# Norms over heads and memory norm inside the q/k/v products, S5 tables on GpSimd, weight splits ahead of an attention

## The chip, the core and the metric

The kernel runs on one core of a Trainium2 chip as one launch. Its time is the device time of that core in microseconds. TensorE (PE) multiplies into eight PSUM banks, ScalarE (ACT), VectorE (DVE) and GpSimd (POOL) compute beside it, SyncE (SP) issues the transfers. All engines are ordered by semaphores alone. Each runs its instructions in program order.

## The reference, cut to what matters

Two transformer blocks over 256 tokens of width 1024 in fp32. The first block: an attention with a relative bias, an MLP, a sparse latent attention, an MLP, a norm. The second: a mixer of RWKV and S5 halves, cross attention to a memory, a gated MLP, differential attention, cross attention again, a mixture of experts. The parts that the change touches:

```python
def memory_cross_attention(h, mem_n, w_q, w_kv, q_gain, k_gain, w_o):
    q = rms_norm_2((h @ w_q).reshape(b, t, MEM_HEADS, MEM_HEAD_DIM), q_gain).astype(F32)      # 4 heads of 256
    k, v = jnp.split(mem_n @ w_kv, 2, axis=-1)                                               # mem_n = rms_norm_2(mem, norm_mem[l])
    k = rms_norm_2(k.reshape(b, m, MEM_HEADS, MEM_HEAD_DIM), k_gain).astype(F32)
...
def diff_attention(h, w_qkv, q_gain, k_gain, lam_q1, lam_k1, lam_q2, lam_k2, sub_gain, w_o, lambda_init):
    q, k, v = jnp.split(h @ w_qkv, 3, axis=-1)
    q = rms_norm_2(q.reshape(b, t, DIFF_HEADS, 2, DIFF_HEAD_DIM), q_gain).astype(F32)        # 16 groups of 64
    k = rms_norm_2(k.reshape(b, t, DIFF_HEADS, 2, DIFF_HEAD_DIM), k_gain).astype(F32)
```

S5 needs cos and sin of (step x angle) for 256 steps and 16 x 128 states; the kernel makes them by doubling a table, level by level.

## The kernel before, in words

The program is a chain of stages (`stage`), each a block with one function per engine and a barrier at its end. A stage's functions are written in the order in which each engine runs them; nothing is scheduled by a planner.

Weights come as tiles of 128 x 2048 fp32 (1 MB) through a ring of six. For precision each is split into a high part (`hi`, L280, ScalarE) and a low part (`lo`, L289, VectorE: tile minus high), two fp32r matrices whose products are added. Split tiles live in `WS`, which has `WS_BUFS = 2` buffers, so the high half of tile i waits until PE has used tile i-2:

```python
                if s >= WS_BUFS:
                    before = [j for j in range(i) if not self.tiles[j][1]][s - WS_BUFS]
                    act.wait_ge(self.filled.sem, self.tile_used[before])
```

`qkv_products` runs eight q/k products (u = 0 to 7, one tile each, 32 matmuls, L459 and L460) and four v tiles (24 matmuls each, L365). Behind product i ScalarE splits tile i+2 and copies the product's part with low activations (L1030), VectorE makes the low half and adds the parts into `qk` (L1042, `bank_copied`).

`grouped_norm` is a stage of its own behind it. ScalarE squares two tiles at a time (L757), PE sums them over the partitions of a head with a matrix of ones (L770, fp32), ScalarE and VectorE make one inverse root a head and token (L761, L789), PE spreads it back over partitions (L781, fp32), VectorE multiplies it with the gain onto q and k (L794). It serves both cross attentions, the differential attention, and others that don't change. A cross attention has ahead of its products: the norm of x (`norm_stage`), a stage that waits for the memory's transfer, and the same `norm_stage` on the memory.

`mlp` runs chunks of up (and gate) and down tiles. In the second MLP of the first block `beside` is the S5 object: `tables_dve` puts steps of the table on VectorE behind each tile, from tile 7 on the doublings (`double`, L2305). The stage of the latent attention that picks the top keys ends with copies on ScalarE and the selection on VectorE; `project`, behind the attention, needs two split tiles of the output weights.

## Time and profile before

| | us |
|---|---|
| median of 3 runs | 2943.56 |
| lowest, highest | 2926.44, 2945.67 |
| the profiled execution | 2930.94 |
| its span | 2929.1 |
| mean granted TensorE clock | 0.937 |
| PE busy | 2601.7 (89%) |
| VectorE, ScalarE, GpSimd busy | 1915.5, 1515.6, 90.4 |

The span is the time between the first and the last record on the core. A busy time is the sum of an engine's records; matmuls overlap, so 89% isn't PE at its peak. The granted clock is given as a share of 2.4 GHz; 0.5 is 1.2 GHz. Line numbers (L280) are those of the kernel before. "idle before" is the time in which an engine waited just ahead of that instruction, with whom it waited for.

### The profile page before, as it was taken

What the parts mean: (1) busy time and instruction counts of PE and PEld (TensorE: products, weight loads), DVE (VectorE), ACT (ScalarE), POOL (GpSimd) and SP (SyncE); (2) the same over time, 40 slices, a digit from 0 to 9 for tenths busy, and PEclk for the clock granted to TensorE, in tenths of its full rate; (3) what the DMA queues carried; (4) which work ended last, traced back from release to release, by engine and by line L of the source; (5) the groups of instructions that cost most, each with busy time, mean ns of one, the idle gap of its engine ahead of it and who ended that gap; (6) DMA issues with size and microseconds to landing.
All of it is one profiled execution on the core that took longest, in us unless ns stands there. A gap on an engine that the chain in (4) does not pass through costs nothing. (4 is left out here: it accounts for less than half of the span.)

```text
span 2929.1 us, 37611 instructions
## 1 busy us (share of the span) xinstructions
PE 2601.7 (89%) x13581; PEld 2117.6 (72%) x13582; DVE 1915.5 (65%) x2368; ACT 1515.6 (52%) x1875; POOL 90.4 (3%) x115
## 2 busy tenths in 40 slices
PE   6889887997869698998978879998998999999998
PEld 5678765776765486887757657777887777777777
DVE  4555545796668544555455459885454889888888
ACT  3544335443221343444444347774443777777776
POOL 0000011000143000000100000000000000000000
PEclk9999988998887898999989879999998999999999
DMA  8346512455200541464414239995554899999996
GB/s 276 133 153 191 164 58 94 144 179 164 68 2 1 201 158 58 159 198 147 144 40 147 72 115 365 327 361 188 183 182 152 313 319 348 330 357 330 358 328 225
DMA packets 333583, 566.24 MB, mean 193 GB/s; under 512 B 21929, under 2 KB 126712, under 8 KB 333080
## 3 DMA queue, kind: packets, MB, share of 16 engines
q1 hardware_dynamic: 333464, 564.59, 56.9%
q8 instruction: 83, 1.36, 0.2%
q14 instruction: 36, 0.29, 0.0%
HBM read 561.19 MB, written 6.50 MB: 194 GB/s over the span
## 5 line engine op out<-in xcount | busy, mean ns | idle before, releaser
L1240 DVE TENSOR_TENSOR weights_split<-ring,weights_split 128x1024 fp32r<-128x1024 f32 x676 | 819.3, 1224 | 266.5 <-ACT weights_split L1235 229.2
L1315 PE MATMUL ps<-weights_split,expert_split 128*128 128x512 f32 x3864 | 914.6, 394 | 25.9 <-DVE expert_split L1411 17.7
L1235 ACT ACTIVATE weights_split<-ring 128x1024 fp32r<-128x1024 f32 x676 | 715.3, 1061 | 353.1 <-PE ps L1315 341.8
L1315 PEld LDWEIGHTS ps<-weights_split,expert_split 128*128 128x128 f32 x3864 | 722.3, 189 | 193.2 <-DVE weights_split L1240 38.2
L289 DVE TENSOR_TENSOR weights_split<-ring,weights_split 128x2048 fp32r<-128x2048 f32 x182 | 413.4, 2272 | 418.0 <-ACT weights_split L280 417.4
L280 ACT ACTIVATE weights_split<-ring 128x2048 fp32r<-128x2048 f32 x182 | 345.0, 1896 | 436.4 <-PE ps L460 259.0
L459 PE MATMUL ps<-normed_split,weights_split 128*128 128x512 f32 x1248 | 446.4, 400 | 25.5 <-PEq L342 25.1
L460 PE MATMUL ps<-normed_split,weights_split 128*128 128x256 f32 x1248 | 353.7, 283 | 0.0
L459 PEld LDWEIGHTS ps<-normed_split,weights_split 128*128 128x128 f32 x1248 | 239.6, 192 | 82.1 <-issue 27.5
L365 PE MATMUL ps<-weights_split,hidden_split 128*128 128x512 f32 x1032 | 244.4, 393 | 17.4 <-DVE weights_split L289 9.3
L460 PEld LDWEIGHTS ps<-normed_split,weights_split 128*128 128x128 f32 x1248 | 239.9, 192 | 1.4
L365 PEld LDWEIGHTS ps<-weights_split,hidden_split 128*128 128x128 f32 x1032 | 191.8, 189 | 61.4 <-issue 12.4
L365 PE MATMUL ps<-weights_split,normed_split 128*128 128x512 f32 (+1 forms) x816 | 197.4, 403 | 26.0 <-DVE normed_split L586 18.8
L365 PEld LDWEIGHTS ps<-weights_split,normed_split 128*128 128x128 f32 x816 | 157.2, 198 | 65.4 <-issue 20.9
L1315 PE MATMUL ps<-weights_split,normed_split 128*128 128x512 f32 x672 | 159.1, 397 | 0.0
L1315 PEld LDWEIGHTS ps<-weights_split,normed_split 128*128 128x128 f32 x672 | 126.1, 189 | 30.2
L527 ACT ACTIVATE hidden_split<-arena 128x512 fp32r<-128x512 f32 x43 | 27.2, 633 | 150.7 <-DVE arena L554 115.5
L365 PE MATMUL ps<-normed_split,weights_split 128*128 128x256 f32 (+2 forms) x576 | 73.3, 291 | 9.1 <-PEq L342 7.5
L365 PEld LDWEIGHTS ps<-normed_split,weights_split 128*128 128x128 f32 (+2 forms) x576 | 72.2, 194 | 10.7 <-issue 8.6
L659 PE MATMUL ps<-const,arena 128*128 128x128 f32 x176 | 38.7, 410 | 44.5 <-DVE arena L640 44.5
L659 PEld LDWEIGHTS ps<-const,arena 128*128 128x128 f32 x176 | 34.7, 217 | 48.8 <-DVE arena L640 48.8
L781 PE MATMUL ps<-arena 8*128 8x256 f32 (+2 forms) x120 | 45.5, 562 | 12.9 <-DVE arena L789 12.9
(393 smaller groups left out, 2339.0 us busy)
## 6 DMA issues: line engine op xcount, KB each, us to landing
ring<-moe_w_gate SPq DMA_DIRECT2D x112, 1024.0 KB, 5.2
ring<-moe_w_up SPq DMA_DIRECT2D x112, 1024.0 KB, 5.3
ring<-moe_w_down SPq DMA_DIRECT2D x112, 1024.0 KB, 5.2
ring<-mlp_w_up SPq DMA_DIRECT2D x32, 1024.0 KB, 5.5
ring<-mlp_w_down SPq DMA_DIRECT2D x32, 1024.0 KB, 5.0
ring<-xa_w_kv SPq DMA_DIRECT2D x16, 1024.0 KB, 5.2
ring<-moba_w_qkv SPq DMA_DIRECT2D x12, 1024.0 KB, 12.2
ring<-da_w_qkv SPq DMA_DIRECT2D x12, 1024.0 KB, 5.2
```

The costliest lines, as they stand in the source:

```text
L280: self.nc.scalar.activation(self.half(i, 0), self.ring_tile(i), ACT.Copy).then_inc(*self.hi_done.up())
L289: self.nc.vector.tensor_tensor(self.half(i, 1), self.ring_tile(i), self.half(i, 0).bitcast(F32), ALU.subtract).then_inc(*self.lo_done.up())
L365: ins = core.nc.tensor.matmul(out, lhs, rhs, start=(first and n == 0), stop=(last and n == len(PASSES) - 1))
L459: core.nc.tensor.matmul(out, w[0][w_at], xs[:, :, k, :], start=first, stop=False)
L460: return core.nc.tensor.matmul(out[:, 0:T], w[1][w_at], xs[:, 0, k, :], start=False, stop=last)
L527: nc.scalar.activation(HS[:, c % 2, 0].rearrange("p k t -> p (k t)"), h[:, c % 2, :], ACT.Copy)\
L659: last = nc.tensor.transpose(core.ps[:, k // 2, k % 2 * T + tt * P:k % 2 * T + (tt + 1) * P], xs[:, tt, k * P:(k + 1) * P], core.c("ident"))
L781: last = nc.tensor.matmul(ps[:, 1 + u % 3, j * T:(j + 1) * T], ones[:, k * P:(k + 1) * P], inv, start=True, stop=True)
L1235: nc.scalar.activation(split_piece(p, 0), ring_piece(p), ACT.Copy).then_inc(high.sem, 1)
L1240: nc.vector.tensor_tensor(split_piece(p, 1), ring_piece(p), split_piece(p, 0).bitcast(F32), ALU.subtract)\
L1315: last = nc.tensor.matmul(ps[:, banks[half][tt], :], stationary(s, k, tt), split_piece(p, i)[:, kk * NW:(kk + 1) * NW], start=(opens and n ...
```

## The change

The two cross attentions and the differential attention use a new function, `qkv_normed`, in place of `qkv_products` and `grouped_norm`. `per_unit == 1` (`one`) is the cross attention, with heads of 256; there VectorE first adds the two squares of a product (`both`, `halves_added`) and PE sums once (`pick`). With heads of 64 PE sums twice. The inverse roots are kept as 32 or 64 rows of a high part above as many of a low one, so that a single fp32r matmul spreads them (`spread_unit`); those of q are made behind product 4, those of k behind the first v tile. In a cross attention the memory is normed at the head of this stage, beside product 0, and transposed by PE behind it; the waiting stage and the memory's `norm_stage` go. In the differential attention the lambda steps lead the stage, and GpSimd makes the slopes' table in it.

The S5 doublings go from VectorE to GpSimd (`tables_pool`), each linked to the one before it. The stage ahead of the latent attention splits two tiles of the output weights at its end.

```diff
         e.dma_start(mem, w["mem_2"][0].rearrange("(t p) d -> p t d", p=P)).then_inc(*mem_landed.up(16))
     norm_stage(core, core.x, core.XS, at_col("norm_xattn_2", 8 * layer), 0, extra_sp=sp)
-    def sp(e):
-        e.wait_ge(*mem_landed.at(0))
-    stage(core, sp=sp)
     qk = a(0, 16 * T).rearrange("p (n t) -> p n t", t=T)
     vN = a(4096, TT * D).rearrange("p (t d) -> p t d", t=TT)
     oT = a(6144, 8 * T).rearrange("p (n t) -> p n t", t=T)
     SCR = 8192
-    with core.scoped("memory_split", [P, 2, KD, T], F32R) as MS:
-        norm_stage(core, mem, MS, at_col("norm_mem_2", 8 * layer), 0)
-        qkv_products(core, core.XS, MS, qk, vN, None)
     def gain(j):
         which, r = at_col("xa_q_gain_2" if j < 8 else "xa_k_gain_2", 2 * layer)
         return core.cols[:, which, r + j % 2:r + j % 2 + 1]
-    gpe, gact, gdve = grouped_norm(core, qk, 16, MD, "norm_xattn", gain, SCR)
-    stage(core, pe=gpe, act=gact, dve=gdve)
+    def mem_gain(k):
+        which, r = at_col("norm_mem_2", 8 * layer + k)
+        return core.cols[:, which, r:r + 1]
+    with core.scoped("memory_split", [P, 2, KD, T], F32R) as MS:
+        qkv_normed(core, 1, gain, qk, vN, (mem, MS, mem_gain, mem_landed))
     q, k = qk[:, 0:8, :], qk[:, 8:16, :]
...
+def qkv_normed(core, per_unit, gain, qk, vN, memory=None, lead=None, pool=None):
...
+    SUMS, SPREAD = 6, (7, 7, 7, 7, 7, 2, 3, 6)
+    v_bank = lambda half, tt: 4 * (1 - half) + tt
+    mem, MS, mem_gain, mem_landed = memory or (None, core.XS, None, None)
...
+    def pe(e):
+        def pick(u):
+            cols = slice(u // 4 * T, u // 4 * T + T)
+            if u == 0 and memory:
+                e.wait_ge(*mem_split.at(4))
+            if u == 4:
+                e.wait_ge(*roots.at(1))
+            if one:
+                e.wait_ge(*halves_added.at(u + 1))
+                first = u % 4 + 1
+                last = nc.tensor.matmul(ps[0:R, SUMS, cols], c("pick_all")[:, PICK - first:PICK - first + R],
+                                        both[:, u % 2, :], start=(u % 4 == 0), stop=(u % 4 == 3))
+            else:
+                e.wait_ge(*squares.at(u + 1))
+                first = 2 * (u % 4)
+                for t in range(2):
+                    last = nc.tensor.matmul(ps[32 * t:32 * t + 32, SUMS, cols],
+                                            c("pick")[:, PICK - first:PICK - first + 32],
+                                            sq[:, u % 2, t * T:(t + 1) * T], start=(u % 4 == 0), stop=(u % 4 == 3))
+            last.then_inc(*sums.up())
...
+        def spread_unit(j):
+            if j == 0:
+                e.wait_ge(*spreader_made.at(1))
+            if j % 4 == 0:
+                e.wait_ge(*inverse_.at(j // 4 + 1))
+            if 1 <= j <= 4:
+                e.wait_ge(*normed.at(j))
+            if j == 5:
+                e.wait_ge(*freed.at(8))
+            if j == 7:
+                e.wait_ge(*roots.at(2))
+            for t in range(2):
+                m = j % 4 if one else 2 * (j % 4) + t
+                last = nc.tensor.matmul(ps[:, SPREAD[j], t * T:(t + 1) * T], spreader[0:2 * R, m * P:(m + 1) * P],
+                                        split[0:2 * R, :], start=True, stop=True)
+            last.then_inc(*spread.up())
+        for u in range(8):
+            w = core.weights(e, t0 + u)
+            xs = core.XS if u < 4 else MS
+            if u >= 2:
...
+            if u == 4 and memory:
+                e.wait_ge(*mem_split.at(4))
+            for t in range(2):
+                for k in range(KD):
+                    last = wide_product(core, ps[:, 2 * (u % 2) + t, :], w, (ALL, k, slice(t * P, (t + 1) * P)),
+                                        xs, k, k == 0, k == KD - 1)
+            core.fill(last, bank=True, tile=True)
+            if u == 0 and memory:
+                for tt in range(TT):
+                    e.wait_ge(*mem_scaled.at(tt + 1))
+                    for k in range(KD):
+                        last = nc.tensor.transpose(ps[:, 4 + k // 2, k % 2 * T + tt * P:k % 2 * T + (tt + 1) * P],
+                                                   mem[:, tt, k * P:(k + 1) * P], c("ident"))
+                        if tt == TT - 1 and k % 2 == 1:
+                            last.then_inc(*mem_turned.up())
+            if u >= 1:
+                pick(u - 1)
+            if u >= 5:
+                spread_unit(u - 5)
+        for i in range(4):
+            half, j = i // 2, i % 2
+            if i == 2:
+                e.wait_ge(*freed.at(8))
+            w = core.weights(e, t0 + 8 + i)
+            for tt in range(TT):
+                for k in range(4):
+                    last = product(core, ps[:, v_bank(half, tt), :], w, (ALL, k, ALL), halves(MS),
+                                   (ALL, 4 * j + k, slice(tt * P, (tt + 1) * P)), j + k == 0, 4 * j + k == 7, tokens=True)
+                if j == 1 or tt == TT - 1:
+                    core.fill(last, bank=(j == 1), tile=(tt == TT - 1))
+            if i == 0:
+                pick(7)
+                spread_unit(3)
+            if i == 1:
+                spread_unit(4)
+            if i == 2:
+                for j in (5, 6, 7):
+                    spread_unit(j)
...
+    def act(e):
+        if lead:
+            lead.act(e)
+        if memory:
+            e.wait_ge(*mem_landed.at(0))
...
+        for i in range(12):
+            core.hi(e, min(t0 + i + 1 + WS_BUFS, t0 + 13))
+            if i < 8:
+                core.wait_bank(e, i)
+                if i >= 2:
+                    e.wait_ge(*freed.at(i - 1))
+                nc.scalar.activation(two(low[:, i % 2, :]), ps[:, 2 * (i % 2):2 * (i % 2) + 2, T:2 * T], ACT.Copy)\
+                    .then_inc(*low_kept.up())
+                e.wait_ge(*freed.at(i + 1))
+                if i >= 2:
+                    e.wait_ge(*(halves_added if one else sums).at(i - 1))
+                nc.scalar.activation(sq[:, i % 2, :], flat(qk[:, 2 * i:2 * i + 2, :]), ACT.Square).then_inc(*squares.up())
...
+            if i == 0 and memory:
+                for b in range(4):
+                    e.wait_ge(*mem_turned.at(b + 1))
...
+            if i == 4:
+                e.wait_ge(*sums.at(4))
+                nc.scalar.activation(root, ps[0:R, SUMS, 0:T], ACT.Sqrt, bias=eps(E_EPS256 if one else E_EPS64, R))\
+                    .then_inc(*roots.up())
+            if i == 8:
+                e.wait_ge(*sums.at(8))
+                nc.scalar.activation(root, ps[0:R, SUMS, T:2 * T], ACT.Sqrt, scale=1.0 / size, bias=eps(E_EPS, R))\
+                    .then_inc(*roots.up())
...
+    def dve(e):
+        def invert(phase):
+            e.wait_ge(*roots.at(phase + 1))
+            core.link(e, "dve", V.reciprocal(inv, root))
+            if phase:
+                e.wait_ge(*spread.at(4))
+            core.link(e, "dve", V.tensor_copy(split[0:R, :], inv))
+            V.tensor_tensor(split[R:2 * R, :], inv, split[0:R, :].bitcast(F32), ALU.subtract)\
+                .then_inc(*inverse_.up())
+        def apply(j):
+            e.wait_ge(*spread.at(j + 1))
+            if one:
+                for t in range(2):
+                    last = V.scalar_tensor_tensor(qk[:, 2 * j + t, :], qk[:, 2 * j + t, :], gain(2 * j + t),
+                                                  ps[:, SPREAD[j], t * T:(t + 1) * T], ALU.mult, ALU.mult)
+            else:
+                last = V.scalar_tensor_tensor(flat(qk[:, 2 * j:2 * j + 2, :]), flat(qk[:, 2 * j:2 * j + 2, :]),
+                                              gain(2 * j), ps[:, SPREAD[j], :], ALU.mult, ALU.mult)
+            last.then_inc(*normed.up())
+        if lead:
...
+        if memory:
+            e.wait_ge(*mem_landed.at(0))
...
+        for i in range(12):
+            core.lo(e, min(t0 + i + 1 + WS_BUFS, t0 + 13))
+            if one and 1 <= i <= 8:
+                u = i - 1
+                e.wait_ge(*squares.at(u + 1))
+                if u >= 2:
+                    e.wait_ge(*sums.at(u - 1))
+                V.tensor_tensor(both[:, u % 2, :], sq[:, u % 2, 0:T], sq[:, u % 2, T:2 * T], ALU.add)\
+                    .then_inc(*halves_added.up())
+            if i < 8:
+                e.wait_ge(*low_kept.at(i + 1))
+                V.tensor_tensor(qk[:, 2 * i:2 * i + 2, :], ps[:, 2 * (i % 2):2 * (i % 2) + 2, 0:T], two(low[:, i % 2, :]),
+                                ALU.add).then_inc(*freed.up())
+            if i == 0 and memory:
+                for b in range(4):
+                    e.wait_ge(*mem_high.at(b + 1))
+                    for j in range(2):
+                        k = 2 * b + j
+                        last = V.scalar_tensor_tensor(MS[:, 1, k, :], ps[:, 4 + b, j * T:(j + 1) * T], mem_gain(k),
+                                                      MS[:, 0, k, :].bitcast(F32), ALU.mult, ALU.subtract)
+                    last.then_inc(*mem_split.up())
+            if i in (4, 8):
+                invert(i // 4 - 1)
+            if 5 <= i <= 9:
+                apply(i - 5)
+            if i == 10:
+                for j in (5, 6, 7):
+                    apply(j)
+    stage(core, pe=pe, act=act, dve=dve, pool=pool, uses=12)
+    guard.__exit__(None, None, None)
...
-        if n == 7:
-            link = self.core.link
-            link(e, "dve", self.core.nc.vector.memset(self.COS[:, :, 0:1], 1.0))
-            link(e, "dve", self.core.nc.vector.memset(self.SIN[:, :, 0:1], 0.0))
-            self.double(e, 1, 0, ST)
-            self.double(e, 2, 0, ST)
-        if n == 8:
-            self.double(e, 4, 0, ST)
-            self.double(e, 8, 0, ST)
-        first = 9
-        for level in self.LEVELS[4:]:
...
+    def tables_pool(self, e):
+        g, link = self.core.nc.gpsimd, self.core.link
+        t1, t2 = self.qt
+        link(e, "pool", g.memset(self.COS[:, :, 0:1], 1.0))
+        link(e, "pool", g.memset(self.SIN[:, :, 0:1], 0.0))
+        e.wait_ge(*self.turn_made.at(1))
+        tt = lambda out, x0, x1, op: link(e, "pool", g.tensor_tensor(out, x0, x1, op))
+        q = (self.co, self.si)
+        for level in self.LEVELS:
             count = min(ST, 512 // level)
-            for group in range(ST // count):
-                for part in range(2):
-                    if n == first:
-                        self.double(e, level, group * count, count, (part,))
-                    first += 1
+            for first in range(0, ST, count):
+                which = slice(first, first + count)
+                x1, x2 = (t[:, 0:count * level].rearrange("p (s n) -> p s n", n=level) for t in self.tmp)
+                qc, qs = bc(q[0][:, which], 2, level), bc(q[1][:, which], 2, level)
+                COS, SIN = self.COS[:, which, :], self.SIN[:, which, :]
+                tt(x1, COS[:, :, 0:level], qc, ALU.mult)
+                tt(x2, SIN[:, :, 0:level], qs, ALU.mult)
+                tt(COS[:, :, level:2 * level], x1, x2, ALU.subtract)
+                tt(x1, COS[:, :, 0:level], qs, ALU.mult)
+                tt(x2, SIN[:, :, 0:level], qc, ALU.mult)
+                tt(SIN[:, :, level:2 * level], x1, x2, ALU.add)
+            if level < self.LEVELS[-1]:
+                q2 = (self.qc, self.qs) if q[0] is not self.qc else (self.qc2, self.qs2)
+                tt(t1, q[0], q[0], ALU.mult)
+                tt(t2, q[1], q[1], ALU.mult)
+                tt(q2[0], t1, t2, ALU.subtract)
+                tt(t1, q[0], q[1], ALU.mult)
+                tt(q2[1], t1, t1, ALU.add)
+                q = q2
...
+        core.hi(e, core.taken + 3 + WS_BUFS)
...
+        core.lo(e, core.taken + 3 + WS_BUFS)
...
-    qkv_products(core, core.XS, core.XS, qk, vN, None)
-    npe, nact, ndve = grouped_norm(core, qk, 16, 64, "norm_diff",
-                                   lambda j: col("da_q_gain_2") if j < 8 else col("da_k_gain_2"), SCR)
...
+    qkv_normed(core, 4, lambda j: col("da_q_gain_2") if j < 8 else col("da_k_gain_2"), qk, vN, lead=Lambda(), pool=pool)
```

The order of the instructions shows how this stands on the engines. The names are those of the tiles (`weights_split` the split weights, `ring` the landed ones, `arena` scratch, `ps` PSUM), and [waits ...] names semaphores. VectorE in the first cross attention's products, kernel before:

```order
L348 UNCONDITIONAL_BRANCH [waits barrier_Pool_Activation_PE_DVE_SP_release]
L289 TENSOR_TENSOR weights_split<-ring,weights_split 128x2048 [waits weights_high]
L1042 SCALAR_TENSOR_TENSOR arena<-ps,arena 128x512 [waits bank_low]
L289 TENSOR_TENSOR weights_split<-ring,weights_split 128x2048 [waits weights_high]
L1042 SCALAR_TENSOR_TENSOR arena<-ps,arena 128x512 [waits bank_low]
```

The same engine there, changed kernel, from the end of product 0's work (L1264 writes the memory's low half; L287 is what L289 was, L1257 what L1042 was):

```order
L1264 SCALAR_TENSOR_TENSOR memory_split<-ps,cols,memory_split 128x256
L287 TENSOR_TENSOR weights_split<-ring,weights_split 128x2048 [waits weights_high]
L1253 TENSOR_TENSOR arena<-arena 128x256 [waits group_squares]
L1257 TENSOR_TENSOR arena<-ps,arena 128x512 [waits bank_low]
L287 TENSOR_TENSOR weights_split<-ring,weights_split 128x2048 [waits weights_high]
```

The add of the squares, L1253, is new and stands between the low half of a tile and the add of that product. PE there, changed kernel, between products 1 and 2 (L457 and L458 are the product's matmuls, L1087 the sum over partitions):

```order
L457 MATMUL ps<-normed_split,weights_split 128x512
L458 MATMUL ps<-normed_split,weights_split 128x256
L1087 MATMUL ps<-arena,const 32x256 [waits group_halves]
L457 MATMUL ps<-normed_split,weights_split 128x512 [waits bank_copied,weights_split]
L458 MATMUL ps<-normed_split,weights_split 128x256
```

L1087 is new between two products, and waits for VectorE's L1253. ScalarE there, changed kernel (L278 is the high half, which waits for PE's `products`, L1175 the low activations' copy, L1180 the square):

```order
L278 ACTIVATE weights_split<-ring 128x2048 [waits products,weights_landed1]
L1175 ACTIVATE arena<-ps 128x512 [waits bank_copied,products]
L1180 ACTIVATE arena<-arena 128x512 [waits group_halves,bank_copied]
L278 ACTIVATE weights_split<-ring 128x2048 [waits products,weights_landed2]
L1175 ACTIVATE arena<-ps 128x512 [waits bank_copied,products]
```

The square is new behind the copy, and waits for VectorE.

## Rows read from the trace of the kernel before

Columns of a timeline row: start, duration in us, engine, line, operation, out<-in by tile, shapes, count, and idle time before it with its releaser. Columns of a window: the stretch, its length, then busy us (instructions) of PE, PEld, DVE, ACT and POOL, mean granted clock, share of the DMA engines, GB/s.

**Rows 1.** The page's costliest groups: busy, mean ns, idle before, releaser
```profile
L280 ACT ACTIVATE weights_split<-ring 128x2048 fp32r<-128x2048 f32 x182 | 345.0, 1896 | 436.4 <-PE ps L460 259.0
...
L460 PE MATMUL ps<-normed_split,weights_split 128*128 128x256 f32 x1248 | 353.7, 283 | 0.0
```
**Rows 2.** Windows: memory norm, norms over heads (cross, differential), attention's start, products
```profile
1015.10:1024.90 9.80, 3.67 (x16) 3.29 (x17) 6.20 (x14) 4.66 (x12) 0.00 (x0) 0.65 0.11 39
1094.20:1119.80 25.60, 21.13 (x64) 12.76 (x64) 9.93 (x18) 5.48 (x9) 0.00 (x0) 0.70 0.11 38
1442.80:1469.60 26.80, 20.49 (x64) 12.43 (x64) 10.66 (x24) 8.19 (x13) 10.04 (x8) 0.74 0.10 36
1119.80:1124.70 4.90, 4.83 (x12) 3.87 (x13) 0.69 (x1) 1.60 (x2) 0.00 (x0) 0.50 0.00 2
1024.90:1093.90 69.00, 68.38 (x352) 58.35 (x352) 30.02 (x19) 27.09 (x23) 0.00 (x0) 0.98 0.47 153
```
**Rows 3.** Timelines of ScalarE, then VectorE, in the cross attention's products
```profile
1037.92 1.92 ACT L280 ACTIVATE weights_split<-ring 128x2048 fp32r<-128x2048 f32 x1 [3.15 <-PE ps L460]
...
1043.47 1.92 ACT L280 ACTIVATE weights_split<-ring 128x2048 fp32r<-128x2048 f32 x1 [3.14 <-PE ps L460]
...
1039.87 2.29 DVE L289 TENSOR_TENSOR weights_split<-ring,weights_split 128x2048 fp32r<-128x2048 f32 x1 [2.65 <-ACT weights_split L280]
1042.08 0.68 DVE L1042 SCALAR_TENSOR_TENSOR arena<-ps,arena 128x512 f32<-128x512 f32 x1
```
**Rows 4.** Timelines: an add of 256 columns, and steps of the norms over heads
```profile
581.16 0.42 DVE L2305 TENSOR_TENSOR arena<-toep,arena 128x256 f32<-128x256 f32 x1
...
1094.93 7.14 PE L770 MATMUL ps<-arena,const 128*8 128x256 f32 x32 [1.64 <-ACT arena L757]
...
1096.00 0.63 ACT L757 ACTIVATE arena<-arena 128x512 f32<-128x512 f32 x1 [0.60 <-PE ps L770]
...
1102.70 1.74 DVE L789 RECIPROCAL arena<-arena 8x256 f32<-8x256 f32 x1 [7.21 <-ACT arena L761]
...
1453.00 1.28 ACT L761 ACT_TABLE_LOAD   x1
1454.30 0.56 ACT L761 ACTIVATE arena<-ps,const 32x256 f32<-32x256 f32 x1
```
**Rows 5.** PE's first product of the cross attention: its first matmul, its window
```profile
1024.91 0.47 PE L459 MATMUL ps<-normed_split,weights_split 128*128 128x512 f32 x1 [3.23 <-PEq L342]
...
1024.90:1032.40 7.50, 7.49 (x34) 6.51 (x35) 0.00 (x0) 0.02 (x1) 0.00 (x0) 0.77 0.01 2
```
**Rows 6.** Timeline of ScalarE: splits ten chunks apart in the two MLPs
```profile
224.69 1.92 ACT L280 ACTIVATE weights_split<-ring 128x2048 fp32r<-128x2048 f32 x1 [2.96 <-PE ps L460]
...
334.69 1.92 ACT L280 ACTIVATE weights_split<-ring 128x2048 fp32r<-128x2048 f32 x1 [2.96 <-PE ps L460]
...
567.41 1.91 ACT L280 ACTIVATE weights_split<-ring 128x2048 fp32r<-128x2048 f32 x1 [2.88 <-PE ps L460]
...
690.00 1.92 ACT L280 ACTIVATE weights_split<-ring 128x2048 fp32r<-128x2048 f32 x1 [2.96 <-PE ps L460]
```
**Rows 7.** Timelines of GpSimd and VectorE, alone and beside each other
```profile
429.79 0.73 POOL L2711 TENSOR_TENSOR dsa<-toep,dsa 128x256 f32<-128x256 f32 x1
...
871.32 0.69 DVE L2483 TENSOR_TENSOR ring<-toep,ring 128x512 f32<-128x512 f32 x1
...
881.99 1.11 POOL L2448 TENSOR_TENSOR ring<-ring 128x256 f32<-128x256 f32 x1
882.61 1.03 DVE L2483 TENSOR_TENSOR ring<-toep,ring 128x512 f32<-128x512 f32 x1
```
**Rows 8.** Timelines around the latent attention: ScalarE's last copy, the projection's start
```profile
427.60 0.60 ACT L2679 ACTIVATE arena<-ps 128x512 f32<-128x512 f32 x1 [1.12 <-PE ps L2869]
...
465.35 2.19 ACT L578 ACTIVATE normed_split<-arena 128x512 fp32r<-128x512 f32 x4 [0.34 <-PEq L342]
...
471.72 1.65 PE L365 MATMUL ps<-weights_split,normed_split 128*128 128x512 f32 x3 [7.14 <-DVE weights_split L289]
```

121 lines of the change are left out of this document (76 added, 45 removed).

## The prediction

> **What bounds the kernel now.** I read the page first. TensorE (PE) is 89% busy and ends nearly every step of the chain that ended last; the costliest ScalarE line, the high half of the weights' split (L280), spends 259 us idle behind PE's L460 [rows 1]. So in product stages PE sets the pace and the other engines have slack. Then I read the stages the change touches, by windows [rows 2]. In the first cross attention the memory norm takes 9.8 us, the q/k/v products 69.0, the norm over heads 25.6. The norm over heads before the differential attention takes 26.8 us. Those norm stages are chains across engines and PE's 21 busy us there are small matmuls. They are what the change wants inside the 69 us. The question is then what a product period leaves free. The timeline of a steady product shows it [rows 3]: ScalarE starts the split of the weights that come two products later when a product ends, at 1037.92, again 5.55 us on; VectorE has made the low half and starts what stands behind it at 1042.08, 4.16 us after the product's end. The two buffers of split weights make this so: the split can't start before the product ends.
>
> **The change, part by part.** *Cross attention (twice), gains.* The two norm stages go: 9.8 + 25.6 = 35.4 us. The scores behind them no longer start on a half clock (4.9 us at 0.50 [rows 2]): half of that, 2.4. Together 37.8.
>
> *Cross attention, costs.* (a) The memory's 16 transposes now stand in the middle of dense PE work: 3.67 us busy in the old stage, at a clock of 0.65 [rows 2], taken as 3.4. (b) The sum matmul of product u-1 stands in PE's queue between products u and u+1, and waits for `halves_added`. The order shows VectorE's add of the two squares, L1253, *behind* the low half of product u+2's weights, which waits for the high half, which waits for product u's end. So PE cannot pass the end of product u before split, add and sum are done. That is 4.16 (to the slot behind the split) + 0.42 (an SBUF add of 256 columns) + 0.45 (one sum: 7.14 us / 16 [rows 4]) + 0.3 for the handovers, an estimate: a high half ends at 1039.84 and its reader starts at 1039.87 [rows 3], and there are several such steps and the matmuls' own filling: 5.35. Behind the waiting sum in the queue stands the whole of product u+1, and behind that every engine. It occurs for u = 1 to 7 and once more behind the first v tile: 8 x 5.35 = 42.8 us. Its cover doesn't exist: the DMA, ScalarE and VectorE are all ahead or waiting for PE. (c) The clock. Before the first product PE sat idle 3.23 us, and that product ran 7.50 us at a mean clock of 0.77, against 5.55 after it at full clock [rows 3, 5]: 1.95 us lost. The new idle spells are 4.7 us long, so I charge 1.95 for each: 15.6 us. Bounds: nothing, and 5.55 (a whole product at 1.2 GHz). (d) 16 spreading matmuls, now single-pass fp32r: a 256-column one lasts 0.28 us [rows 1], overlapped, so about 0.2: 3.0. The old ones are gone with their stage. Squares (0.63), reciprocal (1.74) and the products with gains fit the slack that (b) makes. The sum per cross attention: 3.4 + 42.8 + 15.6 + 3.0 - 37.8 = 27.0, twice 54.0 us.
>
> *Differential attention.* Gone: 26.8, and half of the low clock behind it, estimated at 1.4. Here the squares are summed without L1253, and square u-1 is done 4.16 + 0.68 + 0.63 = 5.5 us after product u-1 [rows 3, 4], before product u ends, so there is no such wait. PE gets 16 sums x 0.45 = 7.1 and 3.0 of spreads. Once, the inverse is late: product 4 ends, then 5.5 to its square, a table load 1.28, root 0.56, reciprocal 1.74, two short copies of some 0.4 each: 9.9 [rows 4]; PE arrives after 5.55 + 2 x 0.89 = 7.3, and waits 2.6 (bounds 0 and 4), for which I take a clock loss of 1.9, and 0.9 at the second inverse. Sum: 7.1 + 3.0 + 2.6 + 1.9 + 0.9 - 28.2 = -12.7. GpSimd's slopes ran under the norm and now run under products that are four times as long.
>
> *S5 tables.* In the MLP without tables ten chunks take 110.0 us (224.69 to 334.69); beside the doublings 122.6 (567.41 to 690.00) [rows 6]. The most to gain is 12.6. GpSimd takes 0.73 us for 256 columns [rows 7], so at most 1.46 for 512; 42 such operations are 61 us, and the 65 smaller ones at about 0.3 another 20. These 81 us fit the ten chunks and the stage's rest if nothing holds them up. But VectorE and GpSimd do hold each other: L2483, an add of two SBUF tiles, takes 0.69 us alone and 1.03 beside a GpSimd operation, whose own time rises from 0.73 to 1.11 [rows 7]. Each chunk has four such VectorE operations (two splits, the squared relu, the hidden split), of which three are in a chain with some 0.6 us to spare; at 0.35 a piece that chain is 1.05 late, 0.45 too much. For about ten chunks: 4.6 us given back. I take -8.0 (bounds -12.6 and +8). The Trainium skill states the same as a lock ("SBUF — State Buffer", SBUF: two separate sides: the pair of ports is held for the whole instruction and the other side blocks). The rows agree with it; by the page alone GpSimd gets only what is left of a chunk by the VectorE operations with two SBUF inputs, and that is rival 3.
>
> *Splits ahead.* ScalarE's last copy of the stage before starts at 427.60 and takes 0.60; two splits behind it, with their low halves, move that stage's end by 5.7 us. The projection's first matmul comes 6.37 us after the stage's first copy (465.35 to 471.72) [rows 8] and can come after 1.5; PE's clock gains half a microsecond and loses one earlier. Net +1.0.
>
> **The sum.** 54.0 - 12.7 - 8.0 + 1.0 = +34.3 us. The profiled execution took 2930.9 us (span 2929.1 and 1.8 around it), which makes 2965.2. That execution is 12.6 us under the median of the runs (2943.56); the four together have a mean of 2936.7. I give the middle of what these suggest, **2970 us**.
>
> **Rivals.**
> 1. *The clock holds across the waits.* Against it: the 7.50 us product. For it: nothing says that a spell of 4.7 us between dense products does what 3.23 us between small ones did. Without 2 x 15.6 and 1.9 the sum is +1: 2938. Chance 0.13.
> 2. *The clock stays low.* Each product behind a wait runs at 1.2 GHz throughout, 5.55 more instead of 1.95, 16 times: +58, 3028. Chance 0.07. The Trainium skill describes such a loop ("TensorE: Matmul & The Clock Gate", HAM oscillation: a wait in each tile makes each burst run cold). The rows show a recovery inside one product.
> 3. *GpSimd becomes the bound of the S5 stage.* Split, relu and hidden split hold VectorE 4 times a chunk; if GpSimd gets less than half of each chunk, its 81 us need over 160, more than the ten chunks and the three or four behind the first turn's end hold, and the 12.6 turn into a loss of about 8: +50, 2986. Chance 0.10.
> 4. *Faster: the sums don't hold PE.* If L1253 were ready when PE comes to the sum, a cross attention would cost 3.4 + 8 x 0.45 + 3.0 - 37.8 = -27.8, and all of it -55.6 - 19.7 = -75: 2861. The sign turns where a sum costs PE less than 5.2 us, clock included (I have 7.3). What speaks against it is the order: the add is queued behind a split that the end of the same product releases. Chance 0.06.
>
> **Numbers.** The forecast has 0.61, with a range of its own of 2950 to 2990 (handovers, the clock term at 1 to 2.5 us a wait, the S5 term). The rivals have 0.36 together, 0.03 is open. For 8 in 10 the range goes down to rival 1 and up past rival 3: 2936 to 2995. It leaves out rivals 2 and 4 and tails. One percent, 29 us, is about what a measurement of this kernel can tell from no change. The forecast's +34 lies just above it: I put 0.43 of its 0.61 over it and 0.18 within. Slower: 0.43 + 0.07 + 0.08 = 0.58. Same: 0.18 + 0.13 + 0.05 = 0.36. Faster: 0.06.
>
> **What would show it.** In the new profile: PE idle some 4.7 us before each L1087 in both cross attentions, released by VectorE's L1253, eight times each, with a period of about 12.9 us between starts of the high halves there against 5.55 before; a clock near 0.8 in that stage, which lasts about 132 us; in the differential attention periods of about 6.4 us and one idle spell before L1111; ten MLP chunks beside GpSimd in about 115 us; the second split done when the projection starts. The prediction is wrong if the high halves in a cross attention come every 6 to 7 us.

## The result and the profile after

| | before | after |
|---|---|---|
| median, us | 2942.56 (4 runs) | 2978.89 (4 runs) |
| lowest, highest | 2926.44, 2945.67 | 2971.95, 2984.31 |
| span of the profiled execution | 2929.1 | 2970.1 |
| mean granted TensorE clock | 0.937 | 0.928 |
| PE busy | 2601.7 | 2590.2 |

The ratio is 1.0134, with a 95% interval of 1.0098 to 1.0170: 36 us slower by the medians, where the sum said +34.3 and the forecast was 2970. The profiled executions differ by 41.0.

PE has less to do than before and ends later, so it waits more. The page's costliest groups of the changed kernel name the wait (columns as in [rows 1]):

```profile
L278 ACT ACTIVATE weights_split<-ring 128x2048 fp32r<-128x2048 f32 x182 | 345.0, 1896 | 478.2 <-PE ps L458 287.5
...
L1087 PE MATMUL ps<-arena,const 128*32 128x256 f32 x32 | 16.9, 631 | 77.9 <-DVE arena L1253 77.9
```

L1087 is the sum over a head in the cross attentions. There are 16 sums (each is recorded as two passes, hence x32), and PE sat idle 77.9 us ahead of them, 4.87 each, all of it for VectorE's add L1253. Here is one of them, in the first cross attention, from the timelines of ScalarE, VectorE and PE (L1180 makes the squares that the add reads, L1111 spreads the inverse roots, L363 are the matmuls of a v tile):

```profile
1092.45 0.63 ACT L1180 ACTIVATE arena<-arena 128x512 f32<-128x512 f32 x1 [2.81 <-DVE arena L1257]
...
1101.06 1.91 ACT L278 ACTIVATE weights_split<-ring 128x2048 fp32r<-128x2048 f32 x1 [7.97 <-PE ps L458]
...
1103.00 2.29 DVE L287 TENSOR_TENSOR weights_split<-ring,weights_split 128x2048 fp32r<-128x2048 f32 x1 [8.44 <-ACT weights_split L278]
1105.21 0.42 DVE L1253 TENSOR_TENSOR arena<-arena 128x256 f32<-128x256 f32 x1
...
1105.68 1.06 PE L1087 MATMUL ps<-arena,const 128*32 128x256 f32 x2 [4.72 <-DVE arena L1253]
...
1106.67 0.79 PE L1111 MATMUL ps<-inverse_norms 64*128 64x256 f32 x2
...
1107.40 7.25 PE L363 MATMUL ps<-weights_split,memory_split 128*128 128x512 f32 x24
...
1114.74 1.91 ACT L278 ACTIVATE weights_split<-ring 128x2048 fp32r<-128x2048 f32 x1 [7.85 <-PE ps L363]
```

The product ends at 1101, ScalarE splits the next weights, VectorE makes their low half, and only then, at 1105.21, comes the add of 0.42 us, whose input had been ready since 1093.08. PE starts its sum 4.6 us after the high half's start and the next product after that. One round takes 13.68 us from high half to high half; in [rows 3] it takes 5.55.

The windows of two such rounds, and of the whole stage, show the clock that goes with it (columns as in [rows 2]). Above them stand two of the product's matmuls of 512 columns in the first of these rounds, one early and one late: the product starts at the lower clock and is back at the full one before it ends.

```profile
1039.50 0.63 PE L457 MATMUL ps<-normed_split,weights_split 128*128 128x512 f32 x1
...
1045.35 0.39 PE L457 MATMUL ps<-normed_split,weights_split 128*128 128x512 f32 x1
...
1033.10:1046.30 13.20, 8.50 (x34) 6.47 (x34) 3.23 (x3) 3.00 (x4) 0.00 (x0) 0.74 0.25 81
1059.70:1073.30 13.60, 8.85 (x34) 6.71 (x34) 5.66 (x6) 3.41 (x5) 0.00 (x0) 0.75 0.25 78
...
1005.20:1139.00 133.80, 94.84 (x391) 72.72 (x390) 47.96 (x60) 35.60 (x42) 0.00 (x0) 0.78 0.24 79
```

To see where the time came and went, the next table takes the starts of the 182 high halves in each trace (180 of them of 1 MB weight tiles) and gives the time between the same two of them. They are the same points of the program in every kernel of this study. "Again" are the two unedited kernels in the ninth and tenth experiment.

| stretch (high halves, from 0) | before | again | after | again |
|---|---|---|---|---|
| second MLP, S5 tables (60 to 86) | 157.3 | 157.3 | 150.6 | 150.6 |
| mixer stages, no edit (86 to 97) | 270.6 | 270.7 | 266.8 | 272.1 |
| first cross attention (97 to 114) | 180.5 | 180.4 | 211.8 | 210.1 |
| differential attention (153 to 163) | 129.9 | 130.8 | 118.2 | 118.3 |
| second cross attention (163 to 179) | 157.5 | 157.5 | 192.6 | 192.6 |

So the two cross attentions cost 31.3 and 35.1 us, the differential attention gives 11.7, the tables 6.7. The projection behind the latent attention and all before it (0 to 53) gives 0.8. The untouched mixer stages give 3.8 in this pair of executions, and the rest, 2.4 us, lies in stages and a mixture of experts that no edit touches.

### The profile page after: what moved, and what is told of

The parts are those of the page before. It is cut to its first block and busy times, and to the rows that moved or that the text cites. A ratio compares the mean times of both kernels' runs of the same rounds, so it can differ in the third digit from the quotient of the medians.

```text
span 2970.1 us, 37411 instructions
## 1 busy us (share of the span) xinstructions
PE 2590.2 (87%) x13501; PEld 2104.7 (71%) x13502; DVE 1899.4 (64%) x2288; ACT 1515.8 (51%) x1878; POOL 207.2 (7%) x224
## 5 line engine op out<-in xcount | busy, mean ns | idle before, releaser
L287 DVE TENSOR_TENSOR weights_split<-ring,weights_split 128x2048 fp32r<-128x2048 f32 x182 | 420.2, 2310 | 520.8 <-ACT weights_split L278 520.7
L278 ACT ACTIVATE weights_split<-ring 128x2048 fp32r<-128x2048 f32 x182 | 345.0, 1896 | 478.2 <-PE ps L458 287.5
L457 PE MATMUL ps<-normed_split,weights_split 128*128 128x512 f32 x1248 | 457.1, 407 | 26.8 <-PEq L340 26.8
L458 PE MATMUL ps<-normed_split,weights_split 128*128 128x256 f32 x1248 | 357.6, 287 | 0.0
L457 PEld LDWEIGHTS ps<-normed_split,weights_split 128*128 128x128 f32 x1248 | 244.5, 196 | 89.0 <-issue 34.1
L363 PE MATMUL ps<-weights_split,hidden_split 128*128 128x512 f32 x1032 | 242.4, 390 | 14.2 <-DVE hidden_split L555 8.1
L458 PEld LDWEIGHTS ps<-normed_split,weights_split 128*128 128x128 f32 x1248 | 244.7, 196 | 1.4
L363 PEld LDWEIGHTS ps<-weights_split,hidden_split 128*128 128x128 f32 x1032 | 190.6, 188 | 56.6 <-DVE hidden_split L555 10.0
L363 PE MATMUL ps<-weights_split,normed_split 128*128 128x512 f32 (+1 forms) x816 | 196.8, 402 | 21.1 <-DVE normed_split L584 21.1
L363 PEld LDWEIGHTS ps<-weights_split,normed_split 128*128 128x128 f32 x816 | 156.3, 197 | 59.9 <-issue 23.3
L1087 PE MATMUL ps<-arena,const 128*32 128x256 f32 x32 | 16.9, 631 | 77.9 <-DVE arena L1253 77.9
L363 PE MATMUL ps<-normed_split,weights_split 128*128 128x256 f32 (+2 forms) x576 | 72.1, 288 | 8.8 <-PEq L340 7.2
L363 PEld LDWEIGHTS ps<-normed_split,weights_split 128*128 128x128 f32 (+2 forms) x576 | 71.0, 190 | 10.3 <-issue 8.3
L2526 POOL TENSOR_TENSOR arena<-arena 128x16 f32<-128x16 f32 (+5 forms) x71 | 67.0, 944 | 5.6
L1087 PEld LDWEIGHTS ps<-arena,const 128*32 128x32 f32 x32 | 2.9, 140 | 83.1 <-DVE arena L1253 60.7
```

Of the source, the lines that this page charges most:

```text
L278: self.nc.scalar.activation(self.half(i, 0), self.ring_tile(i), ACT.Copy).then_inc(*self.hi_done.up())
L287: self.nc.vector.tensor_tensor(self.half(i, 1), self.ring_tile(i), self.half(i, 0).bitcast(F32), ALU.subtract).then_inc(*self.lo_done.up())
L363: ins = core.nc.tensor.matmul(out, lhs, rhs, start=(first and n == 0), stop=(last and n == len(PASSES) - 1))
L457: core.nc.tensor.matmul(out, w[0][w_at], xs[:, :, k, :], start=first, stop=False)
L458: return core.nc.tensor.matmul(out[:, 0:T], w[1][w_at], xs[:, 0, k, :], start=False, stop=last)
L2526: tt = lambda out, x0, x1, op: link(e, "pool", g.tensor_tensor(out, x0, x1, op))
```

## The experiments

**1. The add ahead of the split.** VectorE's add moves from behind the low half to ahead of it; nothing else changes.

```diff
         for i in range(12):
-            core.lo(e, min(t0 + i + 1 + WS_BUFS, t0 + 13))
             if one and 1 <= i <= 8:
                 ...
                 V.tensor_tensor(both[:, u % 2, :], sq[:, u % 2, 0:T], sq[:, u % 2, T:2 * T], ALU.add)\
                     .then_inc(*halves_added.up())
+            core.lo(e, min(t0 + i + 1 + WS_BUFS, t0 + 13))
```

> The changed kernel with VectorE's add of the two squares moved ahead of the low half of the split. My theory (PE waits because the add is queued behind a split that the end of the same product releases): the square is ready 5.5 us after its product's end and the add takes 0.42, so the sum can start about 6.1 us after the product before; PE waits about 0.5 us instead of 4.72, the clock stays up, the high halves come about 7.2 us apart instead of 13.2 to 14.0, and the time falls by some 16 x 6.5 us to about 2875. Rival (the chain square, add, sum is too long wherever it is queued): a wait of 3 us or more stays before each sum and the time stays above 2930.

Measured: 2880.97, ratio to before 0.9811 (0.9759 to 0.9864). VectorE and then PE in a round of its first cross attention, from the timelines:

```profile
1052.32 0.42 DVE L1252 TENSOR_TENSOR arena<-arena 128x256 f32<-128x256 f32 x1 [0.70 <-ACT arena L1180]
1055.12 2.29 DVE L287 TENSOR_TENSOR weights_split<-ring,weights_split 128x2048 fp32r<-128x2048 f32 x1 [2.38 <-ACT weights_split L278]
...
1046.61 0.62 PE L1087 MATMUL ps<-arena,const 128*32 128x256 f32 x2
1053.01 0.62 PE L1087 MATMUL ps<-arena,const 128*32 128x256 f32 x2
```

The add is done at 1052.74, and PE comes to the sum at 1053.01 without any idle time (no bracket behind the row). The steady rounds take 6.3 us, less than the 7.2 expected. In each cross attention two longer ones are left, one at the start, where the memory is awaited (9.7 us), and the one with the inverse root (9.6 and 11.1 us), which waits 2.80 us for the add. That is why the time is 6 us above the 2875 expected. Moving one operation up in one queue was worth 98 us and turned a loss of 36 into a gain of about 60. The rival falls: the chain of square, add and sum is short enough. The group of the sums, which had 77.9 us of idle time before it, now has 11.2:

```profile
L1087 PE MATMUL ps<-arena,const 128*32 128x256 f32 x32 | 10.2, 403 | 11.2 <-DVE arena L1252 11.2
```

**2. The add on GpSimd.** The same add, in a queue that holds nothing else.

```diff
         for i in range(12):
             core.lo(e, min(t0 + i + 1 + WS_BUFS, t0 + 13))
-            if one and 1 <= i <= 8:
-                ...
-                V.tensor_tensor(both[:, u % 2, :], sq[:, u % 2, 0:T], sq[:, u % 2, T:2 * T], ALU.add)\
-                    .then_inc(*halves_added.up())
...
+    def adds(e):
+        for u in range(8):
+            e.wait_ge(*squares.at(u + 1))
+            if u >= 2:
+                e.wait_ge(*sums.at(u - 1))
+            nc.gpsimd.tensor_tensor(both[:, u % 2, :], sq[:, u % 2, 0:T], sq[:, u % 2, T:2 * T], ALU.add)\
+                .then_inc(*halves_added.up())
-    stage(core, pe=pe, act=act, dve=dve, pool=pool, uses=12)
+    stage(core, pe=pe, act=act, dve=dve, pool=adds if one else pool, uses=12)
```

> The changed kernel with the adds of the two squares on GpSimd, which has nothing else in this stage; VectorE's queue holds none. My theory (only the place in the queue matters): an add of 256 columns took GpSimd 0.73 us, 0.3 more than VectorE, so periods of about 7.5 us and about 2880 us in all. Rival (the wait is the price of the handovers, or VectorE's split holds GpSimd up): the sum still waits 2 us or more behind each product, and the time is 2915 or more.

Measured: 2881.76 (one execution). Another engine, an add of 0.74 us instead of 0.42, and the same time: it is the queue, not the operation.

**3. The wait filled.** PE waits as before, but busy.

```diff
+            if u >= 1 and one:
+                e.wait_ge(*mem_split.at(4))
+                for d in range(18):
+                    nc.tensor.matmul(ps[:, 4, :], core.XS[:, 0, d % KD, 0:P],
+                                     core.XS[:, 0, 0:2, :].rearrange("p k t -> p (k t)"), start=True, stop=True)
             if u >= 1:
                 pick(u - 1)
```

> The changed kernel with 18 matmuls of 512 columns (3.9 us at the full clock, their result unused) on PE ahead of each sum but the last one in the cross attentions; the wait for the add stays as long in all, but PE is busy in it. My theory (the wait costs 4.72 us and the clock that falls because of it another 2.4): the granted clock stays at 1.0, periods shrink from 13.7 to about 11.3 us, and the time falls by some 14 x 2.4 = 34 us to about 2945. Rival (the clock falls for another reason): periods stay at 13.7 us and the time at 2979 or above.

Measured: 2952.89 (one execution). Windows of two rounds:

```profile
1047.20:1058.30 11.10, 10.47 (x52) 8.32 (x52) 3.23 (x4) 3.03 (x3) 0.00 (x0) 1.00 0.30 94
1058.30:1069.50 11.20, 10.55 (x52) 8.34 (x52) 3.23 (x4) 3.03 (x3) 0.00 (x0) 1.00 0.29 94
```

The clock is 1.00 and a round takes 11.1 us instead of 13.4. Set beside the same rounds of the changed kernel, the rounds are 2.1 to 2.5 us shorter. So of what the order costs a round, about 4.8 us is the wait (11.1 less the 6.3 of the first experiment) and 2.1 to 2.5 the clock that falls in it: 1.2 GHz for the sum, the spread and part of the next product. The whole came out at -26 instead of -34. Two of the sums had no filling (the last ones). At the first of each stage PE still waits 2.35 us for the memory, and the 18 matmuls behind that wait take 5.85 us instead of 4.27. This is a measurement, not a cure: the first two experiments, which take the wait away, give back 98.

**4. Two sums, no add.** PE sums both squares, as the differential attention does.

```diff
             if one:
-                e.wait_ge(*halves_added.at(u + 1))
+                e.wait_ge(*squares.at(u + 1))
                 first = u % 4 + 1
-                last = nc.tensor.matmul(ps[0:R, SUMS, cols], c("pick_all")[:, PICK - first:PICK - first + R],
-                                        both[:, u % 2, :], start=(u % 4 == 0), stop=(u % 4 == 3))
+                for t in range(2):
+                    last = nc.tensor.matmul(ps[0:R, SUMS, cols], c("pick_all")[:, PICK - first:PICK - first + R],
+                                            sq[:, u % 2, t * T:(t + 1) * T], start=(u % 4 == 0 and t == 0),
+                                            stop=(u % 4 == 3 and t == 1))
...
                 if i >= 2:
-                    e.wait_ge(*(halves_added if one else sums).at(i - 1))
+                    e.wait_ge(*sums.at(i - 1))
...
-            if one and 1 <= i <= 8:
-                ...
-                V.tensor_tensor(both[:, u % 2, :], sq[:, u % 2, 0:T], sq[:, u % 2, T:2 * T], ALU.add)\
-                    .then_inc(*halves_added.up())
```

> The changed kernel without the add: in the cross attentions PE sums the two squares with two matmuls, as in the differential attention. My theory: the sum waits for the square only, which is ready 5.5 us after its product, about when PE comes to it; a second sum costs PE some 0.5 us more. Periods of about 7.0 us, about 2872 us in all. Rival (the sums themselves are what is dear between products): periods above 9 us and 2905 or more.

Measured: 2882.13, ratio 0.9808 (0.9764 to 0.9853). Steady rounds take 6.73 us, 0.43 more than with the add in the right place, which is the price of one more sum. The whole is 10 us above the 2872 expected and equal to the first experiment's, because here the round with the inverse root is shorter (8.1 and 8.2 us, against 9.6 and 11.1 there). That the add saved PE work was true; it saves 0.43 us a product, and cost 7.

**5. The old cross attentions.** The changed kernel with `memory_cross_attention` as before (its two norm stages, `qkv_products`, `grouped_norm`), and the other three parts new.

```diff
+    def sp(e):
+        e.wait_ge(*mem_landed.at(0))
+    stage(core, sp=sp)
...
-    with core.scoped("memory_split", [P, 2, KD, T], F32R) as MS:
-        qkv_normed(core, 1, gain, qk, vN, (mem, MS, mem_gain, mem_landed))
+    with core.scoped("memory_split", [P, 2, KD, T], F32R) as MS:
+        norm_stage(core, mem, MS, at_col("norm_mem_2", 8 * layer), 0)
+        qkv_products(core, core.XS, MS, qk, vN, None)
+    ...
+    gpe, gact, gdve = grouped_norm(core, qk, 16, MD, "norm_xattn", gain, SCR)
+    stage(core, pe=gpe, act=gact, dve=gdve)
```

> The changed kernel with both cross attentions as they were before the change; the other parts stay. My theory (the parts stand for themselves, and only the cross attentions lose): by the two traces the differential attention gives 11.7 us, the S5 tables 6.5 and the splits ahead 1, so about 2922, 20 us under the kernel before. Rival (part of the loss comes from what surrounds the cross attentions, or the other gains depend on them): within 8 us of the kernel before, or above it.

Measured: 2906.83, ratio 0.9889 (0.9858 to 0.9919), 35 us under the kernel before. The sign is right: only the cross attentions lose. The size isn't: 2922 was expected, and the difference of the profiled executions' spans is 26.3 us. Set against the changed kernel, which differs by the cross attentions alone, it says what these cost: 72 us by the medians, 67 by the profiled spans. In its trace the tables' stretch is 150.6 and the differential attention's 118.3, as in the changed kernel; the mixer stages took 263.4, 7.2 less than before. The old cross attentions took 178.3 and 161.7, where the kernel before has 180.5 and 157.5.

**6. The small doublings spread out**, on the kernel before; nothing on GpSimd.

```diff
             self.double(e, 1, 0, ST)
-            self.double(e, 2, 0, ST)
         if n == 8:
-            self.double(e, 4, 0, ST)
-            self.double(e, 8, 0, ST)
-        first = 9
+            self.double(e, 2, 0, ST)
+        if n == 9:
+            self.double(e, 4, 0, ST)
+        if n == 10:
+            self.double(e, 8, 0, ST)
+        first = 11
```

> The kernel before, with the four small S5 doublings on VectorE at tiles 7, 8, 9 and 10, one each, in place of two at tile 7 and two at tile 8; the large ones move two tiles back. Nothing is on GpSimd. Theory one (over half of what the doublings cost on VectorE came where two small ones stood ahead of one split): the ten MLP chunks that took 122.6 us take about 117. Theory two (each VectorE operation costs alike, wherever it stands): 122 us or more.

Measured: 2929.91 (one execution), and 118.7 us for the ten chunks, nearer to the 117 of theory one than to the 122 of theory two. The starts of high halves (one a chunk) show where. First the kernel before, then the changed kernel, then this one:

```profile
584.49 1.92 ACT L280 ACTIVATE weights_split<-ring 128x2048 fp32r<-128x2048 f32 x1 [2.16 <-PE ps L460]
...
608.08 1.92 ACT L280 ACTIVATE weights_split<-ring 128x2048 fp32r<-128x2048 f32 x1 [2.30 <-PE ps L460]
```
```profile
566.72 1.92 ACT L278 ACTIVATE weights_split<-ring 128x2048 fp32r<-128x2048 f32 x1 [2.88 <-PE ps L458]
...
577.72 1.92 ACT L278 ACTIVATE weights_split<-ring 128x2048 fp32r<-128x2048 f32 x1 [2.96 <-PE ps L458]
...
599.72 1.91 ACT L278 ACTIVATE weights_split<-ring 128x2048 fp32r<-128x2048 f32 x1 [2.09 <-PE ps L458]
...
682.58 1.92 ACT L278 ACTIVATE weights_split<-ring 128x2048 fp32r<-128x2048 f32 x1 [3.64 <-PE ps L458]
```
```profile
569.03 1.91 ACT L280 ACTIVATE weights_split<-ring 128x2048 fp32r<-128x2048 f32 x1 [2.88 <-PE ps L460]
...
605.09 1.92 ACT L280 ACTIVATE weights_split<-ring 128x2048 fp32r<-128x2048 f32 x1 [3.08 <-PE ps L460]
...
687.72 1.92 ACT L280 ACTIVATE weights_split<-ring 128x2048 fp32r<-128x2048 f32 x1 [3.30 <-PE ps L460]
```

| | first three chunks | the other seven |
|---|---|---|
| before (567.41 and 690.00 are in [rows 6]) | 40.67 | 81.92 |
| changed kernel | 33.00 | 82.86 |
| this one | 36.06 | 82.63 |

All of the change's 6.7 us comes from the first three chunks, where the small doublings stood two by two ahead of one split and held it up. Most of it is in the first chunk, which took 17.1 us before (567.41 to 584.49) and 11.0 in the changed kernel (566.72 to 577.72). The seven chunks beside the large ones last as long with them on GpSimd as on VectorE. A better spread, with VectorE alone, gives 4.6 us of the 7.7 in the first three chunks, and 3.9 in all.

**7. A version with the waits taken out**: the add ahead of the low half, the inverse root ahead of the copy on ScalarE, and in the cross attentions the first sum one product later.

```diff
             core.hi(e, min(t0 + i + 1 + WS_BUFS, t0 + 13))
+            if i == 4:
+                e.wait_ge(*sums.at(4))
+                nc.scalar.activation(root, ps[0:R, SUMS, 0:T], ACT.Sqrt, ...).then_inc(*roots.up())
             if i < 8:
                 core.wait_bank(e, i)
...
-            if i == 4:
-                e.wait_ge(*sums.at(4))
-                nc.scalar.activation(root, ps[0:R, SUMS, 0:T], ACT.Sqrt, ...).then_inc(*roots.up())
...
-            if u >= 1:
+            if u == 2 and memory:
+                pick(0)
+            if u >= (2 if memory else 1):
                 pick(u - 1)
```

> The changed kernel with VectorE's add ahead of the low half, the first inverse root on ScalarE ahead of the product's copy (in all three attentions), and in the cross attentions the sum of product 0 behind product 2 instead of 1. My theory: beside the first experiment's 2881 this takes away 2.8 us of wait and some 1.3 of clock behind product 5 in each cross attention, as much behind product 1, and 2.0 us of wait and 1.5 of clock in the differential attention: about 2861, 80 under the kernel before. Rival (other waits take their place): 2875 or more.

Measured: 2867.63, ratio 0.9745 (0.9719 to 0.9772). The three attentions' stretches fall to 158.5, 112.9 and 137.9 us (first experiment: 163.1, 116.8, 144.2), 14.8 us in all, where the terms expected add up to 20. The whole is 7 us above the 2861 expected, and under the rival's 2875. The wait for the inverse in the differential attention went from 3.16 us in two pieces (below) to 0.72:

```profile
1390.68 0.47 PE L1111 MATMUL ps<-inverse_norms 128*128 128x256 f32 x2 [0.72 <-DVE inverse_norms L1212]
```

**8. The same, with the add on GpSimd**, as in the second experiment.

> As the run before it, with the adds on GpSimd instead of ahead of the low half on VectorE. My theory: the same within 3 us, about 2860, since neither add is waited for. Rival (an add on VectorE holds up low halves, or one on GpSimd holds up VectorE): they differ by over 6 us.

Measured: 2862.57, ratio 0.9733 (0.9708 to 0.9758). The medians are 5 us apart where 3 was expected, but the intervals of the two versions overlap and each of their stretches differs by less than 1 us (157.9, 113.0, 137.5). They are not told apart. Both are 75 to 80 us under the kernel before, and 111 to 116 under the changed one.

**9 and 10. Both kernels again**, unedited.

> The kernel before once more, unedited, for a second profile. The fifth experiment came out 9 us lower against the kernel before than the difference of the two profiled executions says. Theory one (the first profiled execution of before was a quick one, and the stages between the second MLP and the first cross attention and the experts, which no edit touches, differ from execution to execution): this execution takes about 2942, and the difference of 10 us lies in those stages, not in the ones the change touches, which repeat within 1 us. Theory two (the touched stages themselves vary): they differ by 3 us or more.

> The changed kernel once more, unedited, for a second profile beside the other. Theory one: the cross attention's products and the differential attention's repeat within 1 us of 149.4 and 118.2 us between the high halves that frame them, whatever the whole execution takes. Theory two: they differ by 3 us or more, and the 31.4 and 35.1 us that the two traces give for the two cross attentions can't be told apart.

Measured: 2937.4 and 2977.59. In these pairs the touched stretches repeat within 1 us with one exception: the first cross attention of the changed kernel is 211.8 and 210.1. The old cross attentions vary more than one pair shows. The fifth and sixth experiments have the same code there and take 178.3 and 178.5 us in the first, 161.7 and 160.8 in the second. The stretch that varies holds the old norm over heads: between the high halves that frame it lie 50.1 to 53.2 us, and in either cross attention it can be the short or the long one. In the kernel before, the spreading matmuls of that norm (L781) ran at a mean clock of 0.50 in the first cross attention and 0.63 in the second, and took 14.0 and 11.3 us:

```profile
1104.50:1118.50 14.00, 13.92 (x32) 10.46 (x32) 6.10 (x14) 0.00 (x0) 0.00 (x0) 0.50 0.00 0
1640.50:1651.80 11.30, 11.16 (x32) 8.46 (x32) 6.09 (x14) 0.00 (x0) 0.00 (x0) 0.63 0.00 0
```

So the difference between the 31.3 and the 35.1 us says nothing about the change.

In theory one the varying stretch was to be the mixer stages in the kernel before; there it wasn't (270.6 and 270.7), and the 6.5 us between its two executions lie in the first stages (2.8, before the high half 50) and behind the last high half (2.8). In the changed kernel the mixer stages did vary, 266.8 and 272.1. Windows of the same stage in its two executions, all 584 matmuls of PE in both:

```profile
869.00:960.00 91.00, 73.26 (x584) 49.26 (x584) 68.40 (x100) 19.08 (x30) 23.20 (x22) 0.85 0.21 73
```
```profile
871.00:968.00 97.00, 83.74 (x584) 56.63 (x584) 67.31 (x99) 19.09 (x30) 23.21 (x22) 0.75 0.20 69
```

The same instructions took PE 73.3 us in one and 83.7 in the other, at a clock of 0.85 and 0.75. Single traces of kernels with an untouched mixer are 263.4 to 272.7 us there, so a comparison of two spans can carry up to 9 us from this stage alone.

## Why the prediction was right, point by point

**What bounds the kernel**, and where VectorE's add would be in time: as told. The step "PE cannot pass the end of product u before split, add and sum are done" is the one that decides, and experiments 1 and 2 show it: with the add elsewhere the wait is gone from the steady rounds.

**(b) The wait**, 8 x 5.35 us with an idle spell of 4.7. Measured: 4.72 in nearly all, 5.82 at the first (which waits for the memory's split as well), then 1.06 for the sum where I had 0.45. (The four terms of 5.35 add up to 5.33.) That a sum lasts longer is the low clock again: the same sum takes 0.62 in experiments 1 and 3.

**(c) The clock**, 1.95 us a wait from the first product's 7.50 us. Measured by experiment 3: 2.1 to 2.5 in a round, the slower sum and spread included. The product alone was sized well: the one that starts at 1038.69 ends at 1046.20, 7.51 us later. What I left out is that the sum, and behind it the spread, run at the low clock too. Rival 1 (the clock holds) is out: windows at 0.74 and 0.75. So is rival 2: the product behind a wait takes 1.5 to 2.3 us longer, not 5.55. The Trainium skill's "TensorE: Matmul & The Clock Gate", HAM oscillation, says that a wait in each tile makes the next tile start cold, every time. The trace agrees: each product behind a wait starts at 1.2 GHz (0.63 us for a matmul of 512 columns) and ends at 2.4 (0.39), with 0.74 and 0.75 as the mean of a round.

**(a), (d) and what was removed.** In the first cross attention the eight rounds with a wait take 108.2 us, where the same eight took 44.6 before: 63.7 more. With 0.65 in the round behind them that is 64.3, where (b), (c) and (d) said 61.4. The round with the transposes is 2.7 longer, where (a) said 3.4 (its 16 transposes took 1.91 us). The two stretches that held the old norm stages are 9.5 and 26.5 shorter, 36.0, where I had 37.8. In the second the rounds are 63.9 longer and the old stages gave 32.8, because there the old norm over heads happened to be quick (see experiments 9 and 10). The sum of both is +66.4 against +54.0 forecast, 12 too little: about half lies in the rounds and half in what was removed.

**The differential attention**, -12.7 forecast, -11.7 measured. The squares are in time, as said: high halves 6.30 us apart. The one late step is the inverse. ScalarE, VectorE and PE of the changed kernel there:

```profile
1431.34 1.28 ACT L1191 ACT_TABLE_LOAD   x1
1432.63 0.47 ACT L1191 ACTIVATE arena<-ps,const 64x256 f32<-64x256 f32 x1
...
1433.13 1.75 DVE L1206 RECIPROCAL arena<-arena 64x256 f32<-64x256 f32 x1 [2.48 <-ACT arena L1191]
...
1433.15 0.63 PE L1093 MATMUL ps<-arena,const 128*32 128x256 f32 x4 [1.14 <-ACT arena L1191]
1435.80 0.77 PE L1111 MATMUL ps<-inverse_norms 128*128 128x256 f32 x2 [2.02 <-DVE inverse_norms L1210]
```

PE waits in two pieces, 3.16 us, for which I had 2.6. The first piece I hadn't seen: the sum of product 4 writes into the bank that ScalarE's root reads, and waits for it. The round that holds both waits is 11.64 us (1433.00 to 1444.64).

**The tables**, -8.0 forecast, -6.7 measured, and "ten chunks in about 115 us" against 115.9. The number was close by luck in part, and its reasoning only half right. I spread cost and gain evenly over ten chunks. The trace has the gain in three and a small loss in the seven others. The contention is there. VectorE's groups between 548 and 660 us and the groups of GpSimd's doublings, by form:

```profile
L287 DVE TENSOR_TENSOR weights_split<-ring,weights_split 128x2048 fp32r<-128x2048 f32 x19 | 49.2, 2589 | 26.4 <-ACT weights_split L278 26.3
L555 DVE TENSOR_TENSOR hidden_split<-arena,hidden_split 128x512 fp32r<-128x512 f32 x10 | 8.7, 872 | 7.0 <-ACT hidden_split L525 7.0
...
L2526 POOL TENSOR_TENSOR arena<-arena 128x512 f32<-128x512 f32 x21 | 39.7, 1892 | 1.6
...
L2526 POOL TENSOR_TENSOR arena<-toep,arena 128x512 f32<-128x512 f32 x14 | 20.1, 1437 | 1.1
L2526 POOL TENSOR_TENSOR toep<-arena 128x512 f32<-128x512 f32 x7 | 15.5, 2215 | 0.5
```

A low half takes 2.59 us in the mean against 2.29 alone, the hidden split 0.87 against 0.69. Two of the three groups of 512 columns on GpSimd take 1.9 and 2.2 us in the mean, above the 1.46 that I had as the most; the third takes 1.44. All of its operations there took 117 us, where I had 81. GpSimd was busy to 677 us and not the bound: rival 3 did not come, but it was nearer than I put it.

**The splits ahead**, +1.0 forecast. The latent attention starts 5.8 us later (PE's L836 at 435.11, L838 at 429.31 before), and the projection's first matmul at 472.87 instead of 471.72 [rows 8], with its split tiles ready:

```profile
427.77 3.70 ACT L278 ACTIVATE weights_split<-ring 128x2048 fp32r<-128x2048 f32 x2
...
472.87 7.47 PE L363 MATMUL ps<-weights_split,normed_split 128*128 128x512 f32 x31 [2.27 <-DVE normed_split L584]
```

By the next stage's splits it is 0.8 ahead of before, which is under what two executions differ by. The part does next to nothing: a split done early is paid for where it is done.

**Rival 4** (the sums don't hold PE, 2861) was the right picture of another kernel: experiment 1, where the condition holds, gives 2881, and experiments 7 and 8 give 2868 and 2863.

**How much of it was luck.** The mechanism was right, and its signs are in the trace: sixteen waits of 4.7 to 5.8 us on L1253, rounds of 12.9 to 14.1 us, the stage at 133.8 us. That +34.3 lies so near to +36 is luck in part. The sum of the parts by the traces is +66.4 - 11.7 - 6.7 - 0.8 = +47.2, 13 above the forecast; the untouched stages took 6.2 back in that pair, and the medians say +36. By the medians of the fifth experiment the cross attentions cost 72 us, where I had 54.0, and the rest of the change came with a gain of 35, where I had 19.7: two errors of 15 to 18 us that cancel. Of the second one the traces find nothing in the stages that the change touches (19.2 us there). It lies in stages with the same code in both kernels and in the first profiled execution of before, 11.6 us under its median. Its cause stays open.

## What to carry to other kernels

Before a small step is put into a dense loop, write down for each engine what stands ahead of it in its queue and which event releases that. An operation of 0.42 us whose input is ready costs a whole split and a clock dip, 7 to 8 us, if it is queued behind something that the end of the current product releases; one line higher it costs nothing. Then look at the first and the last turn of the loop (the first sum, the inverse root), which wait for other things than the steady one.
